# Attention with plain transposes, one softmax division per query tile, output products in pieces, and a turned order in the expert blocks

## What is computed

```python
# attention: 8 heads, 64 values each, keys of later 64-row chunks masked
s = (einsum('bqhd,bkhd->bhqk', qn, k_nope) + einsum('bqhd,bkd->bhqk', qp, k_pe)) * MLA_SCALE
mask = k_chunk[None, :] <= (qpos // CHUNK)[:, None]
p = softmax(where(mask[None, None], s, -inf), axis=-1)
attn = einsum('bhqk,bkhd->bqhd', p, val)
...
y = concatenate([attn, gated], axis=-1) @ w_out      # 1024 x 1024
x = layernorm(ALPHA * x + y)
# expert block: the rows of one expert
hid = silu(xb @ w1[e]) * (xb @ w3[e])
acc = acc.at[tok].add((hid @ w2[e]) * wrow[:, None])
```

## Time and profile before

| | |
|---|---|
| median of 3 runs | 1307.57 us (1303.27 to 1307.92) |
| time of the profiled run | 1303.89 us |
| its span | 1302.0 us |
| PE busy, mean granted clock | 1012.3 us (78%), 0.89 of 2.4 GHz |
| first mixer | 0 to 269 us |
| experts of layer 0 | 317 to 571 us |
| attention stage | 751 to 936 us |
| routing of layer 1 | 936 to 985 us |
| experts of layer 1 | 985 to 1259 us |

### The profile page before, as it was taken

How to read it: one execution, slowest core, us unless ns; L and a number is a source line. 1 busy time by engine, 2 the same in 40 slices (tenths; PEclk the granted TensorE clock), 3 DMA queues, 4 the chain that set the end, 5 groups by cost and what they waited for, 6 DMA issues and landing times. The chain is left out here.

```text
span 1302.0 us, 12921 instructions
## 1 busy us (share of the span) xinstructions
PE 1012.3 (78%) x4236; PEld 494.5 (38%) x4236; DVE 438.8 (34%) x1252; ACT 290.9 (22%) x621; POOL 268.6 (21%) x342
## 2 busy tenths in 40 slices
PE   6999999944999987724999777888546898888730
PEld 4444554422333432202455344454432343333310
DVE  0022237443232322237123444442351223222228
ACT  3131211110222211123233422220302222111122
POOL 0000000001233332218101021111003333332218
PEclk9999999975999999975999768997667999999975
DMA  9400040164999999856200090000285999999743
GB/s 345 191 1 1 1 199 1 57 255 183 352 411 410 411 410 411 326 204 208 62 3 6 3 352 20 4 13 17 62 362 184 410 409 411 411 412 384 291 172 140
DMA packets 81943, 276.77 MB, mean 213 GB/s; under 512 B 17498, under 2 KB 21515, under 8 KB 72352
## 3 DMA queue, kind: packets, MB, share of 16 engines
q1 hardware_dynamic: 67424, 253.11, 49.7%
q0 software_dynamic: 10624, 17.93, 3.8%
q10 hardware_dynamic: 3840, 5.00, 1.2%
HBM read 268.04 MB, written 24.72 MB: 225 GB/s over the span
## 5 line engine op out<-in xcount | busy, mean ns | idle before, releaser
L1739 PE MATMUL bank<-l_more,l_e_xT 128*64 128x512 f32 x736 | 171.2, 605 | 26.5 <-DMA l_more<-in_expert_w 26.5
L1695 POOL DMA_INDIRECT y_rows<-l_e_y,l_e_scur x66 | 67.2, 1017 | 313.4 <-DVE l_e_y L1838 313.4
L1832 DVE COPY l_e_hidT<-bank 128x128 f32<-128x128 f32 x66 | 19.2, 291 | 287.4 <-PE bank L1748 287.4
L676 PE MATMUL bank<-shared,m_xT 128*128 128x512 f32 x256 | 114.4, 602 | 1.5 <-ACT m_xp L493 1.5
L1739 PEld LDWEIGHTS bank<-l_more,l_e_xT 128*64 128x64 f32 x736 | 59.3, 139 | 132.3 <-issue 116.0
L1758 PE MATMUL bank<-l_more,l_e_hidT 128*64 128x512 f32 x368 | 90.4, 608 | 23.8 <-issue 19.5
L1801 ACT ACTIVATE l_e_up<-bank 64x512 f32<-64x512 f32 x66 | 39.2, 594 | 294.2 <-PE bank L1739 294.2
L1080 PE MATMUL bank<-shared 128*128 128x512 f32 (+1 forms) x192 | 80.7, 576 | 1.2 <-PEq L131 1.2
L1739 PE MATMUL bank<-shared,l_e_xT 128*64 128x512 f32 x320 | 77.0, 625 | 5.8 <-DMA shared<-in_expert_w 5.8
L1682 POOL DMA_INDIRECT l_e_xg<-x_rows,l_e_gcur x66 | 69.3, 1051 | 52.4 <-POOL l_e_gcur L1679 52.4
L1728 PE MATMUL bank<-ident,l_e_xg 128*128 128x128 f32 x264 | 50.3, 315 | 29.8 <-DMA l_e_xg<-x_rows,l_e_gcur 29.2
(11 more groups left out here) (326 smaller groups left out, 1289.9 us busy)
## 6 DMA issues: line engine op xcount, KB each, us to landing
l_more<-in_expert_w SPq DMA_DIRECT2D x138, 1024.0 KB, 19.2
shared<-in_expert_w SPq DMA_DIRECT2D x60, 1024.0 KB, 18.9
shared<-in_w_in_even SPq DMA_DIRECT2D x4, 2048.0 KB, 17.6
c_y<-y_rows SPq DMA_DIRECT2D x8, 1024.0 KB, 8.3
m_wo<-in_w_out_even SPq DMA_DIRECT2D x1, 4096.0 KB, 27.8
x_rows<-x_tok SPq DMA_DIRECT2D x8, 512.0 KB, 2.7
shared<-in_w_in_odd SPq DMA_DIRECT2D x2, 2048.0 KB, 15.8
m1a_wo<-in_w_out_odd SPq DMA_DIRECT2D x1, 4096.0 KB, 15.2
```

Of the source, the lines that this page charges most:

```text
L676: mm = T.matmul(bank[c % 2][0:n, :], xT[:, k, t * P:t * P + n], w[c][:, k, :], start=(k == 0), stop=(k == KT - 1))
L1695: nc.gpsimd.indirect_dma_start(out=S.y_rows, out_offset=bass.IndirectOffsetOnAxis(ap=scur[:, j:j + 1].bitcast(U32), axis=0), in_=ysb[:, j, ...
L1739: mm = nc.tensor.matmul(bank[2 + j][SLOTS * h:SLOTS * (h + 1), :], xTs[:, j, q, SLOTS * h:SLOTS * (h + 1)], W.w13(at)[:, :, h, q, :], star ...
```

## The change

In the attention:
- `turn(i)` is now a plain transpose of the exp values against the identity; `denominator`, `diag` and all of POOL's instructions are gone. PE waits for ACT's exp instead of POOL.
- `weigh(i)` is done for each head, with the turned exp values as the stationary operand and 64 value columns moving. It follows `turn(i + 1)`. The result lies with query rows on partitions.
- `normalise(t)`, once a tile on DVE, takes 8 reciprocals and multiplies the tile's 8 heads by them. `turn_att(t)` then transposes the result, and ACT copies it.
- The 16 output products of tile t are cut into four pieces of 4, one each in items h = 3 to 6 of tile t + 1, with the gate rows' transposes at h = 1 and the heads' at h = 2. The sample tile has its own operand (`catS`) and bank.
- LayerNorm is class `RowNorm`, as in the first mixer: DVE alone, with 11 small linked instructions in place of ACT's square root. It runs one tile later: `output(t - 1)` at h = 7 of tile t, statistics at h = 1 and the rest at h = 2 of tile t + 1.
- SP issues the fetch of `wo` (4 MB) first, ahead of the LayerNorm's rows.

In the expert blocks the 2 `hid_transposes` stand behind the first of the 4 `x_transposes`, and ACT does silu (`swish`) after the copy of the transposed rows instead of before it.

```diff
@@ PE, attention
-                    pe.wait_ge(g_diag, i + 1)
+                    pe.wait_ge(a_p, i + 1)
...
-                        mm = T.matmul(bank[3 + i % 2][0:rows, b * P:b * P + n], pr[0:n, i % 3, b * P:b * P + rows], diag[0:n, i % 3, 0:n],
-                                      start=(b == 0), stop=(b == len(KB[t]) - 1), skip_group_check=True)
+                        mm = T.transpose(bank[3 + i % 2][0:rows, b * P:b * P + n], pr[0:n, i % 3, b * P:b * P + rows], ident[0:n, 0:n])
...
-                        for e in range(2):
-                            mm = T.matmul(bank[5][MV * e:MV * (e + 1), h // 2 * P:h // 2 * P + n], val[0:rows, slot, (h + e) * MV:(h + e + 1) * MV],
-                                          pT[0:rows, (2 * pair + e) % 4, b, 0:n], start=(h == 0 and b == 0), stop=(h == MH - 2 and b == len(KB[t]) - 1),
-                                          skip_group_check=True)
+                        mm = T.matmul(bank[5][0:n, h * MV:(h + 1) * MV], pT[0:rows, i % 4, b, 0:n], val[0:rows, slot, h * MV:(h + 1) * MV],
+                                      start=(h == 0 and b == 0), stop=(h == MH - 1 and b == len(KB[t]) - 1), skip_group_check=True)
...
                 for i, (t, h) in enumerate(items):
                     if i + 2 < N_ITEMS:
                         scores(i + 2)
                     turn(i)
+                    if i >= 1:
+                        weigh(i - 1)
+                    if t >= 1:
+                        p = t - 1
+                        if h == 1:
+                            if p >= 1:
+                                pe.wait_ge(d_y, p)
+                            turn_u(p, 6)
+                        elif h == 2:
+                            turn_att(p, 7)
+                        elif h == 3:
+                            pe.wait_ge(wo_in, 16)
+                            pe.wait_ge(a_u, p + 1)
+                            products(p, 0, range(4, 8))
...
@@ DVE, attention
+                def normalise(t):
+                    dve.wait_ge(a_p, MH * (t + 1))
+                    link(V.reciprocal(den[0:n, t % 2, :], den[0:n, t % 2, :]))
+                    dve.wait_ge(p_o, MH * (t + 1))
+                    if t >= 1:
+                        dve.wait_ge(p_att, t)
+                    V.tensor_tensor(att[0:n, :, :], bank[5][0:n, :].rearrange("p (h d) -> p h d", h=MH),
+                                    den[0:n, t % 2, :].unsqueeze(2).to_broadcast([n, MH, MV]), ALU.mult).then_inc(d_att, 1)
...
                     turned(i)
+                    if h == 0 and t >= 1:
+                        normalise(t - 1)
+                    if h == 7 and t >= 1:
+                        output(t - 1)
+                    if h == 1 and t >= 2:
+                        ln.statistics(dve, t - 2, ROWS[t - 2], x_tok[:, t - 2, :])
+                    if h == 2 and t >= 2:
...
+                        normed(t - 2)
+                normalise(NT - 1)
+                ln.statistics(dve, NT - 2, P, x_tok[:, NT - 2, :])
+                normed(NT - 2)
                 output(NT - 1)
+                ln.statistics(dve, NT - 1, DEC, x_tok[:, NT - 1, :])
+                normed(NT - 1)
@@ PE, expert blocks
-                    x_transposes(b + 2, 0)
-                    hid_transposes(0)
+                    x_transposes(b + 2, 0, between=hid_transposes)
                     down_products(b, 0, r)
```

More of the change, by code:

```diff
@@ L1229, in weigh, with turn_u @@
                     mm.then_inc(p_o, 1)
-                def gated(t):
+                def turn_u(t, into):
                     n = ROWS[t]
[L1234 to L1237, removed]
                     for k in range(4):
[L1239 to L1248, removed]
+                        mm = T.transpose(bank[into][:, k * P:k * P + n], u[0:n, t, k * P:(k + 1) * P], ident[0:n, 0:n])
+                    mm.then_inc(p_u, 1)
+                def turn_att(t, into):
+                    n = ROWS[t]
+                    pe.wait_ge(d_att, t + 1)
+                    for k in range(4):
+                        mm = T.transpose(bank[into][:, k * P:k * P + n], att[0:n, 2 * k:2 * k + 2, :].rearrange("p h d -> p (h d)"), ident[0:n, 0:n])
+                    mm.then_inc(p_att, 1)
@@ new lines, in products, with sample_products @@
+                def products(t, h, rows):
+                    n = ROWS[t]
+                    for k in rows:
+                        mm = T.matmul(bank[6 + h][0:n, :], catP[:, k, 0:n], wo[:, k, h * HALF:(h + 1) * HALF], start=(k == 4), stop=(k == 3))
+                    return mm
+                def sample_products(rows):
+                    for k in rows:
+                        for q in range(4):
+                            mm = T.matmul(bank[2][DEC * q:DEC * (q + 1), 0:256], catS[:, k, :], wo[:, k, q * 256:(q + 1) * 256], start=(k == 4), stop=(k == 3))
+                    return mm
@@ L1250, in _ @@
                 scores(0)
                 scores(1)
-                for i in range(N_ITEMS):
+                for i, (t, h) in enumerate(items):
                     if i + 2 < N_ITEMS:
                         scores(i + 2)
-                    if i >= 2 and i % 2 == 0:
-                        weigh(i // 2 - 1)
                     turn(i)
-                    if tile_before(i, OUT_AT) is not None:
-                        gated(tile_before(i, OUT_AT))
-                        heads(tile_before(i, OUT_AT))
@@ L1261, in _ @@
-                gated(NT - 1)
-                weigh(N_ITEMS // 2 - 1)
-                heads(NT - 1)
+                    if i >= 1:
[12 more added lines that the diff above has]
+                            products(p, 0, range(4, 8))
+                        elif h == 4:
+                            pe.wait_ge(a_att, p + 1)
+                            products(p, 1, range(4, 8))
+                        elif h == 5:
+                            products(p, 0, range(0, 4))
+                        elif h == 6:
+                            products(p, 1, range(0, 4)).then_inc(p_y, 1)
@@ L1265, in _ @@
+                LAST = NT - 1
+                pe.wait_ge(a_p, N_ITEMS)
+                turn_u(LAST, 0)
+                weigh(N_ITEMS - 1)
+                pe.wait_ge(a_u, NT)
+                sample_products(range(4, 8))
+                turn_att(LAST, 1)
+                pe.wait_ge(a_att, NT)
+                sample_products(range(0, 4)).then_inc(p_y, 1)
             @block.scalar
@@ L1328, in turned @@
                     if i >= 4:
[L1329 removed]
+                        dve.wait_ge(p_o, i - 3)
                     if t < 4:
```

125 lines of the change are left out of this document (50 added, 75 removed).

## The result

The changed kernel takes 1266.87 us (median of 4 runs, 1264.38 to 1269.19) against 1305.42 us of the kernel before on the same chip: a ratio of 0.9716, with a 95% interval of 0.9695 to 0.9738. It is 38.5 us faster by the medians, 37 by the ratio. A second set of runs of the same kernel, among the experiments, gave 0.9713 (0.9696 to 0.9730).

The account below looks back on a forecast made before the run. It took a chain of handovers, not a full engine, to bound the attention, and weight transfers the second expert stage. From 1303.9 us, 27 less in the attention and 2 in the experts gave 1275, range 1260 to 1292.

Parts of the forecast that it names:

- PE's items: Attention: scores, turns and `weigh` per item take 1.19, 1.79, 2.37 us (tiles 1-3) and 0.73 (sample tile).
- PE's stands: Attention: PE waits for DVE's extras 1.0, 4.5, 3.5 and 5.0 us in tile 1, 2, 3 and sample tile.
- The clock: Attention: half clock after three PE waits of 4 to 5 us adds 1.3 us each, 4 us in all.
- The tail: End of the attention: DVE's list of 17.3 us, then 1.4 to the next stage: 18.7 us, where it was 14.
- The experts: Expert blocks, both layers: three transposes behind the hidden ones cover DVE's copy, saving 2 us in all (0 to 4).
- 1 us shorter each: Sign in the expert stages: each should be 1 us shorter, with the DMA share unchanged.
- price of 0.4 us for a block: Expert blocks: covering DVE's copy saves 0.4 us before the down products, counted only where transfers don't hide it.
- Stands with half clock into the pieces: Rival, attention: DVE's extras cost more, one piece and an item at half clock in three tiles, 15 us: 1290; chance 0.20.
- No stands: Rival, attention: DVE gets a head start, the clock never falls; 9 us stands and 4 clock go: 1262; chance 0.16.
- `weigh` at 0.45: Rival, attention: the unpacked `weigh` stays at 0.45 us and longer PE waits come with it: 1308, no gain; chance 0.05.
- Half clock through all items: Rival, attention: the clock stays at half through all items of tiles 1 to 4, +53 us less 4: 1324; chance 0.03.
- `wo` was not waited for: Attention, tile 1: the 4 MB fetch, wanted some 18 us later, is covered narrowly; waiting for it would show the forecast wrong.

Follow-up runs that it names:

- spread: The changed kernel with DVE's LayerNorm statistics moved from h = 1 to h = 3 and finishing passes from h = 2 to h = 5: 1260.40 us, 0.9670.
- late_output: spread with DVE's residual moved from h = 7 to behind the division at h = 0, gate rows' transposes from h = 1 to h = 2: 1259.59 us.
- experts alone: The kernel before with only the expert blocks' part of the change, attention as before: 1299.44 us, 0.9978.
- the late pair: late_output against the same kernel with expert blocks in the old order: 1259.59 us (0.9661) against 1265.38 us (0.9700).
- turn_twice: The changed kernel with every transpose of exp values issued twice into the same place: 1266.45 us, 0.9723.
- turn_product: The changed kernel with exp values turned by a float32 product with the identity instead of a transpose, twice the records: 1267.94 us, 0.9743.
- spread_product: spread and turn_product together, against the changed kernel: 1265.17 us, 0.9701.
- attn_only: The changed kernel with the expert blocks as before, so the attention part alone: 1268.4 us, 0.9746.
- light_experts: light_before with the turned order in the expert blocks; results differ, for time alone: 1245.56 us, 0.9549.
- light_before: The kernel before, fetching only a quarter of w1 and w3 for each block after the first six experts; for time alone: 1267.24 us, 0.9715.

## Why the prediction was right, and where its terms were off

The forecast was 1275 us, from 1260 to 1292; 1266.87 lies in the range, 8 us below the forecast. The direction held, and so did the mechanism in the main: the waits for `diag` are gone, and what is left are stands of PE at DVE's extras. The sum is nearer than its terms: items priced too dear and too cheap in part made up for each other. The difference lies in the size of single terms:

| term | predicted, us | in the trace after, us |
|---|---|---|
| up to the first `turn` | 2.1 | 1.8 |
| tile 0 | 9.6 | 8.8 |
| tile 1, with stands | 24.7 + 1.0 | 25.0 |
| tile 2 | 29.5 + 4.5 | 32.9 |
| tile 3 | 34.2 + 3.5 | 35.7 |
| sample tile | 21.0 + 5.0 | 28.9 |
| tail | 18.7 | 17.8 |
| clock | 4 more | inside the tiles |
| sum | 157.8 | 150.9 |

- **PE's items.** Predicted 1.19, 1.79 and 2.37 us for tiles 1 to 3; at the full clock they last 1.04 (767.87 to 768.91), 1.59 (798.33 to 799.92) and 2.13. Each row's length in the timeline holds the tail of its last instruction, and the prediction added such lengths for the transposes (0.60 for 4, where 0.43 is start to start). Eight items in each of three tiles: 4.7 us too much. The price that had no row, `weigh` at 0.225, came out at 0.21, so it was right to follow the clock. In the sample tile the items were dearer than 0.73 (1.05), some 2.6 us too little.
- **PE's stands.** 14 us predicted, 8.6 found. The prediction put them all at h = 2. The first and longer part (5.3 us) comes at h = 0, where `weigh` waits for the division; it takes its time out of the later wait. DVE's row in tile 2 ran from 782.58 until PE could go on at 794.12, 11.5 us where 12.9 were summed. PE's own work beside it lasted 8.6 us, 8.5 were summed; but 1.7 of it is half clock behind the first stand, and at full clock it would be 6.9. So the agreement of 8.6 with 8.5 is luck: the items were priced too dear and the half clock made up for it. The step that failed is the one that named a single place and added the waiting for the first scores to it. That the statistics and passes make the wait at h = 2 is shown by `spread`, that the residual makes most of the one at h = 0 by `late_output`.
- **The clock.** 4 us predicted. Half clock fills 13.6 us of tiles 2, 3 and the sample tile, which costs at most 6.8; 1.7 of it is in each of tiles 2 and 3, and 2.9 is the one piece of 6.64 us. Before, half clock filled 62 us of the stage (granted clock 0.83), after 29 and 24 in the two traces (0.90 and 0.92), tile 0 and the tail with it. How much of the 34 us of the stage came as clock, and how much as waits, no run separates: the forecast never priced the two apart, as it added up the new stage at full clock.
- **The tail.** 18.7 predicted, 17.8 found, the list of DVE as summed. As forecast it is now longer than before: what the change gives back.
- **The experts.** 2 us predicted, with 0 to 4. Three comparisons give 2.8 (experts alone), 3.9 (attention alone against the whole) and 5.1 us (the late pair), with intervals of 2.5, 5.0 and 4.4 us to each side. So the term was right in kind; the three values lie above 2, but each interval takes it in. In single traces it can't be read: the two expert stages together, first up product to last down product, last 511.9 to 517.6 us in the three traces of the old order and 510.6 to 515.6 in the nine of the new. "1 us shorter each" was a sign that one trace could not have shown. The price of 0.4 us for a block was 0.30. The wait of 0.43 us was put down to DVE's copy; the profile names nothing that PE waited for there, and only its disappearance in the turned order speaks for the copy. Where in the stage the 3 to 5 us appear was not found.

**The rivals.** Stands with half clock into the pieces (1290) happened in the sample tile and, more briefly, in tile 3, not at 5 us in each of three tiles. No stands (1262) was not reached even by `spread`: it still has 5.3 us of them and 6.8 us of half clock in the sample tile, so its 1260.40 us agree with that number by luck, as its items are cheaper than the forecast's. `weigh` at 0.45 did not come. Half clock through all items did not come: tile 1 ran at 1.00, and `turn_twice` shows that transposes as such don't bring it in tiles 1 to 3. `wo` was not waited for.

What stays argued, not shown: how the 34 us of the stage divide between the handover by `diag`, the cheaper turning, the LayerNorm without ACT and the clock, since only the pieces and the experts were taken out by themselves; that spreading the extras keeps the clock up, for which only the count of six tiles against six speaks; and what makes the clock fall after one stand and not after an equal one.

## What to carry to other kernels

Where an engine with an in-order list serves another's items, count its extra work (norms, divisions, residuals) as a row, and put each part beside a long piece of the other engine's work. Here that was worth 5 us beyond the change by moving two steps, most of it as clock, while swapping two extras with nothing to cover them gained nothing. A gain on an engine whose stage is bound by transfers is worth what the transfers leave of it: here 3 to 5 us of some 20. When items are summed from a timeline, take start to start, not the lengths of the rows.

## What the runs showed of the hardware

- 8.3 us of additional PE work in tiles 1 to 3 was taken in by PE's stands for 2.5 us (`turn_product` against the changed kernel) and 2.6 us (`spread_product` against `spread`). The tiles became 2.3 and 5.7 us longer; the 3.4 between is half clock that the changed kernel had and `turn_product` had not.
- One stretch of half clock of 3.4 us cost 1.7 us: tile 3, with the same waits, lasted 35.7 us with it (changed kernel) and 34.0 without (`attn_only`).
- A float32 product with full 128x128 weights and 64 moving columns takes 0.21 us start to start at 2.4 GHz (two records). With 50 moving columns at 1.2 GHz two records took 0.45. The price followed the clock: in tile 2 of the changed kernel three such products took 789.13 - 787.82 = 1.31 us at half clock and 792.20 - 791.58 = 0.62 us at the full clock.
- Equal waits of 2.26 us behind the same instructions were followed at once by 3.4 us of half clock in the changed kernel (the `weigh` took 1.51 us) and not in `spread` or `attn_only` (0.85).
- With each transpose of exp values issued twice, PE stayed at the full clock through tiles 1 to 3 (`turn_twice`, 1.00).
- Splitting a row of four transposes in two cost 0.2 us: 404.59 - 404.27 + 405.53 - 404.97 = 0.88 us in `light_experts` against 406.08 - 405.40 = 0.68 us in `light_before`. That is why less than the whole wait of 0.43 us is gained.
